# Query and key transposes beside the last products, latents behind the first scores, split fp32r products for the second attention

## What is computed

```python
h = rms_norm(x, ln1_g)                         # 512 x 1024
z = h @ w_in                                   # 512 x 1440
q_a, k_a, v_a, c_q, c_kv, k_rope = split(z)    # 512, 128, 128, 384, 256, 32 columns
q_a, k_a = rms_norm per head                   # 8 and 2 heads of 64
o_a = window_gqa(q_a, k_a, v_a, ...)           # first attention, blocks of 128, window of 3 blocks
q  = rms_norm(c_q) @ w_qb                      # latents 384 -> 768
kv = rms_norm(c_kv) @ w_kvb                    # latents 256 -> 1024
o_b = latent attention of q, kv, k_rope        # second attention, 8 heads over all 512 tokens
x = x + [norm(o_a), norm(o_b)] @ w_o
```

## Time and profile before

| | us |
|---|---|
| three runs | 1563.24, 1563.38, 1558.12 |
| their median | 1563.24 |
| the profiled execution, its own time | 1559.61 |
| its span, first to last instruction | 1557.8 |
| TensorE busy, share of the span | 1459.2, 94% |
| VectorE, ScalarE busy | 616.2, 490.8 |
| mean granted clock of TensorE, full is 1 | 0.978 |

### The profile page before, as it was taken

How to read it: one execution, slowest core, us unless ns; L and a number is a source line. 1 busy time by engine, 2 the same in 40 slices (tenths; PEclk the granted TensorE clock), 3 DMA queues, 4 the chain that set the end, 5 groups by cost and what they waited for, 6 DMA issues and landing times.

```text
span 1557.8 us, 17583 instructions
## 1 busy us (share of the span) xinstructions
PE 1459.2 (94%) x7133; PEld 956.3 (61%) x7133; DVE 616.2 (40%) x1188; ACT 490.8 (32%) x904; POOL 69.4 (4%) x96
## 2 busy tenths in 40 slices
PE   8988988998999999999996999988898999999998
PEld 6855466454433433333323899966686888888886
DVE  5366666334122222122115542125675443254325
ACT  6355376331001101100103412357734333123321
POOL 2000000000000000000001200000001101000100
PEclk9989999999999999999998999989999999999999
DMA  7477350427999999999995122140021332233211
GB/s 231 81 306 280 131 208 1 149 104 283 423 420 422 421 421 421 421 421 422 421 421 201 41 89 75 55 162 1 10 86 54 109 108 76 87 108 108 101 35 54
DMA packets 82738, 310.27 MB, mean 199 GB/s; under 512 B 7188, under 2 KB 43309, under 8 KB 55906
## 3 DMA queue, kind: packets, MB, share of 16 engines
q1 hardware_dynamic: 80656, 305.34, 50.2%
q10 hardware_dynamic: 1202, 2.15, 1.2%
q0 software_dynamic: 800, 1.66, 0.3%
HBM read 303.35 MB, written 5.78 MB: 198 GB/s over the span
## 4 chain that ended last, share of the span: by engine, by line
PE 73%; DMA 14%; DVE 6%; ACT 5%; issue 1%; SPq 0%; DVEq 0%; ACTq 0%
PE ps L433 13%; PE ps L434 13%; PE ps L435 13%; PE ps L805 13%; DMA sb<-in_w_gate 5%; DMA sb<-in_w_up 5%; PE ps L663 4%; DMA sb<-in_w_down 2%; PE ps L932 1%; PE ps L757 1%; DMA raw<-in_a_w_in 1%; ACT sb L1068 1%; PE ps L530 1%; PE ps L574 1%; PE ps L620 1%
## 5 line engine op out<-in xcount | busy, mean ns | idle before, releaser
L805 PE MATMUL ps<-sb 128*64 128x512 f32 x1536 | 352.5, 599 | 15.7 <-DMA sb<-in_w_gate 5.4
L805 PEld LDWEIGHTS ps<-sb 128*64 128x64 f32 x1536 | 102.9, 136 | 222.2 <-issue 178.6
L1068 ACT ACTIVATE sb<-ps 128x512 f32<-128x512 f32 (+4 forms) x176 | 90.7, 530 | 342.5 <-PE ps L757 88.3
L434 PE MATMUL ps<-r_fl,r_top 128*128 128x512 f32 x344 | 135.1, 393 | 0.0
L435 PE MATMUL ps<-r_act,r_low 128*128 128x512 f32 x344 | 134.8, 392 | 0.0
L433 PE MATMUL ps<-r_act,r_top 128*128 128x512 f32 x344 | 134.3, 390 | 0.0
L2096 DVE TENSOR_TENSOR r_low<-raw,r_top 128x2048 fp32r<-128x2048 f32 x33 | 74.2, 2289 | 78.7 <-ACT r_top L1068 78.7
L1874 DVE TENSOR_TENSOR sb<-sb,ps 128x512 f32<-128x512 f32 x64 | 43.7, 687 | 139.6 <-PE ps L794 139.6
L433 PE MATMUL ps<-r_low,r_h 128*128 128x256 f32 x288 | 82.5, 287 | 1.0 <-ACT sb L1068 1.0
L1068 ACT ACTIVATE r_top<-raw 128x2048 fp32r<-128x2048 f32 x33 | 61.4, 1907 | 69.7 <-PE ps L435 69.7
L434 PE MATMUL ps<-r_low,r_h 128*128 128x256 f32 x288 | 82.3, 286 | 0.0
(11 more groups left out here) (396 smaller groups left out, 2382.4 us busy)
## 6 DMA issues: line engine op xcount, KB each, us to landing
sb<-in_w_gate SPq DMA_DIRECT2D x64, 1024.0 KB, 25.3
sb<-in_w_up SPq DMA_DIRECT2D x64, 1024.0 KB, 26.0
sb<-in_w_down SPq DMA_DIRECT2D x64, 1024.0 KB, 26.4
sb<-in_w_mod SPq DMA_DIRECT2D x16, 1536.0 KB, 9.1
raw<-in_f_w_up SPq DMA_DIRECT2D x22, 1024.0 KB, 7.6
raw<-in_a_w_in SPq DMA_DIRECT2D x12, 1024.0 KB, 5.4
raw<-in_f_w_down SPq DMA_DIRECT2D x5, 2048.0 KB, 7.8
raw<-in_w_in SPq DMA_DIRECT2D x3, 1440.0 KB, 16.5
```

The lines of the kernel that those rows point to most:

```text
L434: pe.matmul(o, a_hi, b_lo, start=False, stop=False)
L805: mm = pe.matmul(PS[64 * hf:64 * hf + 64, b * HALF:(b + 1) * HALF], lhsT(k), ring[c % RINGN][:, kk, hf * HALF:(hf + 1) * HALF], start=(k = ...
L1068: return act_(o, i_, ACT.Identity, bias=bias, scale=scale)
```

## The change

The change has three parts. (a) Of the transposes of queries and keys, those of token tiles 0 to 2 (15) are issued ahead of the last 18 matmuls of the first projection, those of tile 3 (5) behind them; ScalarE and VectorE copy them out ahead of the last steps of the latents' norm, and two of the four copies of the keys go to VectorE. (b) The latents' 20 transposes move into the first attention: blocks 5 to 7 behind the scores of step 0, blocks 8 and 9 behind those of step 2 (in step 1). They use banks 5 to 7, which `mod_rows` needs next. ScalarE copies each to fp32r (`cT`), VectorE makes the remainder (`cTl`). (c) `w_qb` and `w_kvb` are split in four halves: ScalarE rounds (`wq_h`) in steps 2 to 5, ahead of its copies `ptA_a`; VectorE makes the remainders (`wq_l`) at the end of steps 3 to 6. The projections of the second attention become split products of these. `w_o` shares memory with the split operands, and its transfer waits for the last of those projections.

```diff
@@ TensorE, first projection @@
+                    if half == 1 and k == KD - 1:
+                        for j in range(5):
+                            b = nb(("T", j), *((("qT_" + "da"[j % 2], j),) if j < 4 else (("kz", 1), ("kz_d", 3))))
+                            for t in range(NT - 1):
+                                pe.wait_ge(*at("zqk", t))
+                                pe.transpose(bank(b)[:, t * P:(t + 1) * P], zqk[:, t, j * P:(j + 1) * P], ident)
...
-            for j in range(10):
-                freed = ("qT_" + "da"[j % 2], j) if j < 4 else ("kz", 3) if j == 4 else ("cT", j - 5)
-                b = nb(("T", j), freed)
...
+            pe.wait_ge(*at("zqk", NT - 1))
+            for j in range(5):
+                pe.transpose(bank(bank_of["T", j])[:, (NT - 1) * P:S], zqk[:, NT - 1, j * P:(j + 1) * P], ident).then_inc(*inc("pe_T", j))
+
+            def turn_latents(js):
+
+                for j in js:
+                    b = claim(5 + (j - 5) % 3, ("cTl", j - 5))
+                    bank_of["T", j] = b
+                    for t in range(NT):
+                        if j == 5:
+                            pe.wait_ge(*at("zc", t))
+                        tr = pe.transpose(bank(b)[:, t * P:(t + 1) * P], zr[:, t, (j - 4) * P:(j - 3) * P], ident)
+                    tr.then_inc(*inc("pe_T", j))
...
             a_scores(0)
-            for r in range(3):
-                claim(5 + r, ("modrow", r))
+            turn_latents((5, 6, 7))
+            pe.wait_ge(*at("z_a", (3, 1)))
             pe.wait_ge(*at("csil"))
...
                 if b < 7:
                     a_scores(b + 1)
+                if b == 1:
+                    turn_latents((8, 9))
+                    for r in range(3):
+                        claim(5 + r, ("modrow", r))
                 if b in (1, 2, 4, 5, 7):
                     mod_rows((1, 2, 4, 5, 7).index(b))
...
-                        mm = pe.matmul(bank(x, 384), cqT[:, k, t * P:(t + 1) * P], w_qb[:, k, c * 384:(c + 1) * 384],
-                                       start=(k == 0), stop=(k == 2))
+                        mm = split_product(bank(x, 384), cqT_hi[:, k, t * P:(t + 1) * P], cqT_lo[:, k, t * P:(t + 1) * P],
+                                           wqb_hi[:, k, c * 384:(c + 1) * 384], wqb_lo[:, k, c * 384:(c + 1) * 384], k == 0, k == 2)
...
@@ ScalarE @@
+            def turned_queries():
+
+                eng.wait_ge(*at("qcols"))
+                for j in (1, 3):
+                    eng.wait_ge(*at("pe_T", j))
+                    copy(qTa[:, j, :], bank(bank_of["T", j]), scale=qcolA).then_inc(*inc("qT_a", j))
+                eng.wait_ge(*at("pe_T", 4))
+                for e in range(2):
+                    copy(kz[64 * e:64 * e + 64, 0, :], bank(bank_of["T", 4])[0:64, :],
+                         scale=col2[0:64, C_AK:C_AK + 1]).then_inc(*inc("kz", e))
...
                      accum_out=st[:, t, 12:13]).then_inc(*inc("zsqC", t))
+                if t == NT - 1:
+                    turned_queries()
                 eng.wait_ge(*at("stC_e", t))
...
+                if b == 0:
+                    turned_latents((0, 1, 2))
                 if b < 7:
                     a_exp(b + 1)
+                if b == 1:
+                    turned_latents((3, 4))
+                if 2 <= b < 6:
+                    i, c = W_HALF[b - 2]
+                    eng.wait_ge(*at(("w_qb", "w_kvb")[i]))
+                    copy(W_HI[i][:, c], W_RAW[i][:, c]).then_inc(*inc("wq_h", b - 2))
...
@@ VectorE @@
                     ve.tensor_scalar(t_, t_, esA[:, 4 * b + i:4 * b + i + 1], None, ALU.mult).then_inc(*inc("Ap", (b, i)))
+                if b == 1:
+                    latents_rest((3, 4))
                 for i in (0, 2):
...
+                if b == 0:
+                    latents_rest((0, 1, 2))
+                if 3 <= b < 7:
+                    i, c = W_HALF[b - 3]
+                    eng.wait_ge(*at("wq_h", b - 3))
+                    ve.tensor_tensor(W_LO[i][:, c], W_RAW[i][:, c], W_HI[i][:, c].bitcast(F32), ALU.subtract).then_inc(*inc("wq_l", b - 3))
...
@@ SP @@
+            sp.wait_ge(*at("pe_kv", (3, 1)))
             sp.dma_start(w_o, I["w_o"].rearrange("a (k p) n -> p (a k) n", p=P)).then_inc(*inc("w_o", 0, 16))
```

More of the change, by code:

```diff
@@ L491, in _ @@
                             mm.then_inc(*inc("pe_z", (t, c)))
-            for j in range(10):
-                freed = ("qT_" + "da"[j % 2], j) if j < 4 else ("kz", 3) if j == 4 else ("cT", j - 5)
-                b = nb(("T", j), freed)
-                for t in range(NT):
-                    if j == 0:
-                        pe.wait_ge(*at("zqk", t))
-                    if j == 5:
-                        pe.wait_ge(*at("zc", t))
-                    src = zqk[:, t, j * P:(j + 1) * P] if j < 5 else zr[:, t, (j - 4) * P:(j - 3) * P]
-                    tr = pe.transpose(bank(b)[:, t * P:(t + 1) * P], src, ident)
-                tr.then_inc(*inc("pe_T", j))
+            pe.wait_ge(*at("zqk", NT - 1))
[10 more added lines that the diff above has]
+                    tr.then_inc(*inc("pe_T", j))
             pe.wait_ge(*at("qT_d", 2))
             pe.wait_ge(*at("qT_a", 3))
-            pe.wait_ge(*at("kz", 3))
+            pe.wait_ge(*at("kz", 1))
+            pe.wait_ge(*at("kz_d", 3))
             pe.wait_ge(*at("z_a", (3, 1)))
@@ L566, in _ @@
             pe.wait_ge(*at("cT", 4))
-            pe.wait_ge(*at("w_qb"))
-            pe.wait_ge(*at("w_kvb"))
+            pe.wait_ge(*at("wq_l", 3))
+            pe.wait_ge(*at("cTl", 4))
             turn[0] = 0
@@ L579, in _ @@
                     for k in range(2):
-                        mm = pe.matmul(bank(x), cqT[:, 3 + k, t * P:(t + 1) * P], w_kvb[:, k, c * HALF:(c + 1) * HALF],
-                                       start=(k == 0), stop=(k == 1))
+                        mm = split_product(bank(x), cqT_hi[:, 3 + k, t * P:(t + 1) * P], cqT_lo[:, 3 + k, t * P:(t + 1) * P],
+                                           wkv_hi[:, k, c * HALF:(c + 1) * HALF], wkv_lo[:, k, c * HALF:(c + 1) * HALF], k == 0, k == 1)
                     mm.then_inc(*inc("pe_kv", (t, c)))
@@ L1126, in _, with turned_latents @@
             eng.wait_ge(*at("rs1"))
+            def turned_queries():
[7 more added lines that the diff above has]
+                         scale=col2[0:64, C_AK:C_AK + 1]).then_inc(*inc("kz", e))
+            def turned_latents(js):
+                for j in js:
+                    eng.wait_ge(*at("pe_T", 5 + j))
+                    copy(cqT_hi[:, j, :], bank(bank_of["T", 5 + j]), scale=col1[:, C_CQ + j:C_CQ + j + 1]).then_inc(*inc("cT", j))
             for t in range(NT):
@@ L1151, in _ @@
                 copy(zr[:, t, 512:768], zr[:, t, 512:768], scale=st[:, t, 11:12]).then_inc(*inc("zc", t))
-            eng.wait_ge(*at("qcols"))
-            for j in (1, 3):
-                eng.wait_ge(*at("pe_T", j))
-                copy(qTa[:, j, :], bank(bank_of["T", j]), scale=qcolA).then_inc(*inc("qT_a", j))
-            eng.wait_ge(*at("pe_T", 4))
-            for n in range(4):
-                g, e = divmod(n, 2)
-                copy(kz[64 * e:64 * e + 64, g, :], bank(bank_of["T", 4])[64 * g:64 * g + 64, :],
-                     scale=col2[64 * g:64 * g + 64, C_AK:C_AK + 1]).then_inc(*inc("kz", n))
             def a_exp(b):
@@ L1596, in _ @@
                 ve.tensor_scalar(zr[:, t, 2 * ZCH - QKW:ZR], bank(bank_of["z", t, 2], ZCH), rs[:, t:t + 1], None, ALU.mult).then_inc(*inc("z_d", (t, 2)))
+                if t == NT - 1:
+                    for j in (0, 2):
+                        eng.wait_ge(*at("pe_T", j))
+                        ve.tensor_scalar(qTa[:, j, :], bank(bank_of["T", j]), qcolA, None, ALU.mult).then_inc(*inc("qT_d", j))
+                    eng.wait_ge(*at("pe_T", 4))
+                    for e in range(2):
+                        ve.tensor_scalar(kz[64 * e:64 * e + 64, 1, :], bank(bank_of["T", 4])[64:128, :],
+                                         col2[64:128, C_AK:C_AK + 1], None, ALU.mult).then_inc(*inc("kz_d", 2 + e))
                 eng.wait_ge(*at("zsqC", t))
@@ L1633, in sum_a, with latents_rest @@
                                  ALU.add).then_inc(*inc("sumA", n))
+            def latents_rest(js):
+                for j in js:
+                    eng.wait_ge(*at("cT", j))
+                    ve.scalar_tensor_tensor(cqT_lo[:, j, :], bank(bank_of["T", 5 + j]), col1[:, C_CQ + j:C_CQ + j + 1],
+                                            cqT_hi[:, j, :].bitcast(F32), ALU.mult, ALU.subtract).then_inc(*inc("cTl", j))
             eng.wait_ge(*at("bias_in"))
```

26 lines of the change are left out of this document (13 added, 13 removed).

## The result

The changed kernel takes 1568.53 us (median of 8 runs, 1566.25 to 1570.51), the kernel before on the same chip 1560.92 (8 runs, 1558.12 to 1564.99): ratio 1.0045, 95% interval 1.0035 to 1.0055, or 7.6 us slower. The profiled execution took 1568.30 us, its span is 1566.5, its mean granted clock 0.978 as before. The span grew by 8.7 us, the first `b_scores` came 7.9 us later. So the loss lies in the front, as forecast, and the rest of the program only moved with it, but for 0.8 us.

What follows compares the result with a forecast made beforehand. TensorE carries 73% of the chain, and what counts is when it reaches the first `b_scores`. Terms +6.1 + 3.9 - 2.9 = +7.1 us on 1563.24 gave 1570, range 1561 to 1576.

Steps and rivals of the forecast that it cites:

- signs named for the profile: Expected in the trace after: TensorE idle 4 to 5 us ahead of first mod_rows, ScalarE waits about 1.6 us, among others.
- (a): Ahead of first attention: transposes push the projection's end 1.74 us; first scores at 87.9 instead of 89.06, gain 1.2 us.
- (b) The claim: Step 1: TensorE waits for latents 3 and 4, mod_rows(0) starts at 108.0; with (a) +6.1 us at step 3's scores.
- (c) The roundings: Steps 2 to 5 of first attention: ScalarE's roundings lie on the loop, +3.9 us, bounds 2.5 and 4.3.
- (c) The products: Second attention's projections: shorter split products, VectorE sets the pace, b_heads(0) 3.7 us earlier; net -2.9 us, bounds -3.7 and -1.
- The sum: Whole kernel: +6.1 + 3.9 - 2.9 = +7.1 us, giving 1570 on the median's footing.
- Clock: Rival: after idling at first scores, claim and b_heads, TensorE runs at 1.2 GHz; +11 us, 1574; chance 0.25.
- Slack: Rival: in first attention's loop, ScalarE's roundings and latent copies fall in unneeded idle time; +1 us, 1564; chance 0.15.
- The products bring nothing: Rival: in the projections, split weight loads pace 384-column matmuls at 0.22 us; +9 us, 1572; chance 0.06.
- All of the claim's wait is hidden: Rival: step 1's claim costs nothing, only gains of (a) and (c) stand; -4 to -8 us, about 1557; chance 0.04.

Runs made afterwards that it cites:

- warm_claim: Changed kernel with five useless float32 matmuls of 512 columns ahead of the claim in step 1; 1568.20 us, ratio 1.0043.
- round_behind: Changed kernel with ScalarE's four roundings behind its copies of the value products instead of ahead of the turned probabilities' copies; 1565.76 us, ratio 1.0030.
- late_and_behind: Changed kernel with the claim and first mod_rows moved to step 2 and ScalarE's roundings behind the copies of the value products; 1563.10 us, ratio 1.0004.
- claims_apart: late_and_behind with 15 transposes back behind the last product and both engines' work on blocks 8 and 9 behind step 1's copies; 1558.73 us, ratio 0.9987.
- warm_both: Changed kernel with the useless matmuls of both warm_claim and warm_heads; 1568.85 us, ratio 1.0040.
- warm_heads: Changed kernel with six useless float32 matmuls, four between the halves of mod_rows(6) and two behind it; 1569.34 us, ratio 1.0048.
- latents_first: Changed kernel with blocks 8 and 9 turned ahead of step 2's scores and scaled by ScalarE ahead of its exponentials; 1566.22 us, ratio 1.0022.
- float_products: Changed kernel with second attention's projections as float32 products with raw weights, without the weights' roundings and remainders; 1573.79 us, ratio 1.0079.
- claim_late: Changed kernel with the claim of banks 5 to 7 moved from step 1 to 2, mod_rows in steps 2, 3, 4, 5, 7; 1565.58 us, ratio 1.0015.

## Why the prediction was right, step by step

**The forecast** of 1570 (1561 to 1576) stands 1.5 us above the measured 1568.53, the forecast difference of +7.1 us beside a measured +7.6. That 1570 lies above and +7.1 below what was measured comes from the footing: the three runs of before had a median of 1563.24, the eight beside the changed kernel 1560.92. The signs named for the profile came: the idle ahead of the first `mod_rows`, released by VectorE, the waits of 1.6 us in the steps, VectorE's pace in the projections and the gap ahead of `b_heads`. The terms are not all as good as the sum.

**(a)** 87.9 was forecast for the first scores, 87.17 measured. The push by the 15 transposes can be read within the trace:

```profile
76.81 1.80 PE L494 MATMUL ps<-sb 128*128 128x128 f32 x15
```

The next product starts at 78.36 and the one behind it 0.31 us later instead of 0.22. That is 1.64 us in all, 0.11 a transpose, near the forecast 1.74. VectorE's last copy started only 1.23 us later than before (82.56), since this execution's products ran some 0.4 us ahead. ScalarE's four copies (forecast to end at 87.7) ended at 86.97.

**(b) The claim**, the dear term: place, releaser and queue were right. ScalarE had the two latents from 105.11 to 106.35, VectorE the remainders from 105.81 to 107.22; forecast for `mod_rows(0)` was 108.0, or 107.25 with the 0.75 us for the faster scores off, measured 107.32. What was mis-sized is the next term: `mod_rows(0)` was taken at full clock (2.7 us), and it ran at a granted clock of 0.50, the level that the earlier trace rows show at 91 us before, and took 5.35 us. So at the scores of step 3 the loss was not +6.1 but +8.5, over the upper bound of +8, which was the bound for exactly this case. The addition was off too: the terms as printed (+6.85, less 0.75, less 0.4) give +5.7, and the 2.6 us of half clock would lift that to +8.3. The scores of steps 3 and 7 in the kernel before, which no group above has:

```profile
106.56 1.56 PE L520 MATMUL ps<-sb 64*128 64x384 f32 x8
...
137.00 1.13 PE L520 MATMUL ps<-sb 64*128 64x256 f32 x8
```

**(c) The roundings.** Forecast +3.9. From the scores of step 3 to those of step 7 the changed kernel takes 149.39 - 115.10 = 34.29 us; before, it took 30.44 (137.00 - 106.56): +3.85. Each rounding measured 1.15 or 1.04 us (forecast 1.14 and 1.01), the next operation starting 1.05 or 0.95 us after it did. The four steps grew by 1.06, 1.04, 0.95 and 0.80 us, so three lay on the loop in full and the last nearly. The Trainium skill (ScalarE: Activation LUTs, What ACT_TABLE_LOAD costs) gives such an operation without pointer operands 186 ns + 0.833 ns a column, 1.146 us for 1152; the measured 1.15 agrees.

**(c) The products.** From 162.36 to 164.96 lie 15 starts of 384 columns, 0.173 us each; from 165.13 to 166.99 eight of 512, 0.233 each; forecast 0.172 and 0.229. The Trainium skill (TensorE: Matmul & The Clock Gate, Back-to-back issue gap) gives 0.163 for a lone one of 384 and speaks of some 0.131 sustained at 512; the trace does not bear out the latter for these split products. VectorE set the pace, as forecast: TensorE waited for it (0.47 us at 183.49) and it ended 199.84 - 161.90 = 37.9 us into the stage (forecast 37.5). The piece of `w_mod` landed after 33.0 instead of 31.5; here too the addition was off, for the prediction's own 5 us taken from the 37.7 of before give 32.7. `b_heads` started at +38.0: -3.3 us, forecast -3.7. From there to `b_scores` I had added 0.8 us for more half clock; but `b_heads` took 1.95 us at full clock, where it had taken 2.97, and 1 us came off instead. Net of the stage -4.35 instead of -2.9.

**The sum** as measured: +8.5 + 3.85 - 4.35, with 0.1 us less between, gives the +7.9 at `b_scores`. Two errors, both on the clock, had opposite signs: +2.6 at `mod_rows(0)` (5.35 against 2.7) and -1.9 behind the projections (1.1 off instead of 0.8 on). That the sum was hit to half a microsecond is partly this luck. Nor is the +2.6 a loss that could be had back by itself, for `warm_claim` took it away and its time stayed.

**The rivals.** *Clock*: its first part came true (TensorE at half clock behind the wait), its second did not. At 1574 it was too high by its loss at `b_heads`. At 107 the granted clock was 0.50 behind 5.42 us of idle, and `warm_claim`, where TensorE was kept busy, has 2.78 us and 1.00 at the same place. The rule that the default is throttled and activity releases it (the Trainium skill, TensorE: Matmul & The Clock Gate, What's actually happening) agrees with these two rows. *Slack* falls by the steps' +3.85 and by `round_behind`, where the wait ahead of the value products is gone. *The products bring nothing* falls by 0.173 us. *All of the claim's wait is hidden* falls by the 5.42 us.

**What the change loses** is lost by the order in which parts (b) and (c) put the work. `late_and_behind` differs from the changed kernel in nothing but the place of the claim, of `mod_rows` and of the roundings, and it is level with the kernel before (1.0004 against 1.0045). `claims_apart`, with the latents out of the way of step 1's copies too and the 15 transposes back behind the products, is 9.1 us faster than the change by the ratios. Of part (a), the transposes beside the products brought nothing measurable in time.

## What to carry to other kernels

A wait for a bank stands in TensorE's program in front of everything behind it: find the engine that frees the bank and what stands ahead of that in its program, place the claim a step after the freeing, and keep that work from standing ahead of awaited copies. Put elementwise work that nobody awaits soon behind the copies for which TensorE waits in the same step. The two together were worth 6.4 us here, and 9.1 with the last 2.87 us of such a wait gone; what the roundings' place wins by itself is hardly above the noise. Then look at the transfers: the earlier front met pieces of `w_mod` that had not landed, and lost some 3 us to them. And don't count a saving until the whole is timed, since work at half clock further on may take it back.

## What the runs showed of the hardware

Half-clock work moves about. Where it was taken out of one place of the changed kernel (5.35 us of `mod_rows(0)`, in `warm_claim` and `warm_both`), it appeared in another: at `b_heads` in the one, from 126 to 134 us in the other. Both end at the same first `b_scores`, within 0.15 us. The idle ahead of a row does not say at which level it runs. Ahead of the transposes of step 3 TensorE was idle for 2.78 us in eight of these traces. The same 12 matmul instructions then took 1.51 us before the change, in the changed kernel and in `warm_heads`, 1.69 in `latents_first`, 1.99 in `round_behind`, 2.42 in `warm_both`, and 2.79 in `warm_claim` and `float_products`.

A row of matmuls that is too long need not be at half clock. `mod_rows` took 3.70 us instead of 2.78 in `round_behind` at a granted clock of 1.00, for a piece of its weights; only the granted clock and the split of the row by halves tell the two apart.

The spread of one kernel's runs goes with its mean granted clock. Of the 12 runs of `claims_apart` the two fastest took 1554.1 and 1554.8 us with clock 0.985, the four slowest 1562.3 to 1563.0 with 0.973 to 0.975 (though two at 1558.8 and 1559.1 also had 0.976 and 0.974); those of `claim_late` fall into five at 0.981 to 0.984 (1559.7 to 1561.9) and six at 0.975 to 0.977 (1565.6 to 1568.5). That is more than most single edits here are worth, so one profiled execution says where the time lies but not by how much the median moves.
